# Two of four weight-quarter sums of a seven-product matrix block are made by accumulating DMAs, and modulation rows get four slots instead of two

## The reference, cut to what matters

```
def swiglu_2(h, w_gu, w_down):
    gu = h @ w_gu
    g, u = jnp.split(gu, 2, axis=-1)
    return (jax.nn.silu(g) * u) @ w_down

for l in range(DEPTH_2):
    mod = (c_act @ w_mod[l] + b_mod[l]).reshape(c.shape[0], N_MOD, D_MODEL)
    h = modulate(x, g_norm[l, 0], mod[:, 0], mod[:, 1])
    x = x + 0.5 * mod[:, 2][:, None, :] * swiglu_2(h, w_ffn1_gu[l], w_ffn1_down[l])
    ...                                   # the mixer
    x = x + 0.5 * mod[:, 8][:, None, :] * swiglu_2(h, w_ffn2_gu[l], w_ffn2_down[l])
```

## Time and profile before

| | |
|---|---|
| time, median of 3 runs (range) | 3084.52 us (3080.36 to 3085.5) |
| profiled execution's own time / its span | 3084.16 us / 3082.3 us |
| TensorE busy, share of span | 2865.6 us, 93% |
| VectorE busy | 2375.7 us, 77% |
| ScalarE busy | 1440.6 us, 47% |
| GpSimd busy | 344.7 us, 11% |
| mean granted TensorE clock | 0.978 |
| up halves, first product copied to first down matmul | 211.0, 209.0, 207.6, 209.1 us |
| down halves, first to last down matmul | 149.3, 143.6, 143.0, 120.8 us |

### The profile page before, as it was taken

The page is one execution under the profiler, slowest core; times in us unless marked ns, Lnnn a source line. Parts: engine busy times, 40 slices in busy tenths (PEclk is TensorE's granted clock), DMA queues, the critical chain, the costliest instruction groups (busy, mean ns, idle before and its releaser), DMA issues. The chain is left out here.

```text
span 3082.3 us, 46400 instructions
## 1 busy us (share of the span) xinstructions
PE 2865.6 (93%) x16536; PEld 2396.9 (78%) x16536; DVE 2375.7 (77%) x2913; ACT 1440.6 (47%) x1741; POOL 344.7 (11%) x393
## 2 busy tenths in 40 slices
PE   8999888999999999999989999998999989999998
PEld 4876557777777778897767799876998767789986
DVE  7757758999999978887758688877888666588843
ACT  4125437888888845442146433314333125454421
POOL 0100013333333310101100000010000100000000
PEclk9989999999999999999999999999999999999999
DMA  8552247999999992225631222374223752122221
GB/s 319 169 188 96 90 165 282 368 361 375 373 359 360 368 355 83 95 92 177 235 126 58 80 96 95 117 251 152 94 95 107 252 189 75 63 96 95 94 97 68
DMA packets 115857, 555.68 MB, mean 180 GB/s; under 512 B 20656, under 2 KB 22192, under 8 KB 73776
## 3 DMA queue, kind: packets, MB, share of 16 engines
q1 hardware_dynamic: 89264, 491.43, 43.5%
q0 software_dynamic: 26496, 62.96, 5.7%
HBM read 549.10 MB, written 37.75 MB: 190 GB/s over the span
## 5 line engine op out<-in xcount | busy, mean ns | idle before, releaser
L178 DVE TENSOR_TENSOR stream_low<-stream_raw,stream_high 128x2048 fp32r<-128x2048 f32 x156 | 357.4, 2291 | 254.1 <-ACT stream_high L173 156.0
L173 ACT ACTIVATE stream_high<-stream_raw 128x2048 fp32r<-128x2048 f32 x75 | 143.4, 1913 | 452.7 <-DMA stream_raw<-in_ffn_dn 264.2
L727 ACT ACTIVATE stream_high<-stream_raw 128x2048 fp32r<-128x2048 f32 x76 | 145.5, 1914 | 372.2 <-DVE stream_raw L847 372.2
L473 PE MATMUL ffn_ps_psum<-ffn_t_high,stream_high 128*128 128x256 f32 x912 | 266.8, 293 | 54.6 <-ACT area_f L710 54.6
L473 PE MATMUL ffn_ps_psum<-ffn_pure_high,stream_high 128*128 128x512 f32 x704 | 285.4, 405 | 23.9 <-DVE ffn_pure_low L892 21.5
L317 DVE TENSOR_TENSOR expert_low<-expert_raw,expert_high 128x2048 fp32r<-128x2048 f32 x128 | 292.9, 2289 | 6.3 <-ACT expert_high L313 3.2
L474 PE MATMUL ffn_ps_psum<-ffn_pure_low,stream_high 128*128 128x512 f32 x704 | 278.5, 396 | 0.0
L475 PE MATMUL ffn_ps_psum<-ffn_pure_high,stream_low 128*128 128x512 f32 x704 | 278.1, 395 | 0.0
L475 PE MATMUL ffn_ps_psum<-ffn_t_high,stream_low 128*128 128x256 f32 x912 | 260.9, 286 | 0.0
L474 PE MATMUL ffn_ps_psum<-ffn_t_low,stream_high 128*128 128x256 f32 x912 | 260.8, 286 | 0.0
L313 ACT ACTIVATE expert_high<-expert_raw 128x2048 fp32r<-128x2048 f32 x128 | 244.6, 1912 | 20.4 <-PE experts_g_psum L475 20.4
(11 more groups left out here) (540 smaller groups left out, 7633.8 us busy)
## 6 DMA issues: line engine op xcount, KB each, us to landing
expert_raw<-in_exp_gu SPq DMA_DIRECT2D x128, 1024.0 KB, 9.1
stream_raw<-in_ffn_gu SPq DMA_DIRECT2D x88, 1024.0 KB, 4.8
expert_raw<-in_exp_dn SPq DMA_DIRECT2D x64, 1024.0 KB, 10.7
con<-in_w_mod SPq DMA_DIRECT2D x120, 512.0 KB, 4.3
stream_raw<-in_ffn_dn SPq DMA_DIRECT2D x44, 1024.0 KB, 6.5
mix_mod_rows<-in_w_ada POOLq DMA_DIRECT2D x32, 512.0 KB, 4.4
stream_raw<-in_w_in SPq DMA_DIRECT2D x16, 1024.0 KB, 6.0
pieces_raw<-in_w_in SPq DMA_DIRECT2D x11, 1024.0 KB, 6.3
```

What stands on the lines that cost most here:

```text
L173: self.nc.scalar.activation(self.high[:, q], self.raw[:, q], ACT.Copy).then_inc(self.high_done, 1)
L178: self.nc.vector.tensor_tensor(self.low[:, q], self.raw[:, q], self.high[:, q].bitcast(F32), ALU.subtract)\
L473: mm(out, w[0], x[0], start=start, stop=False)
L727: a(w.high[:, w.slot(s)], w.raw[:, w.slot(s)], ACT.Copy).then_inc(w.high_done, 1)
```

## The change

It has two parts, both in `gated_layer`.

First, the sums. The signs of the scheme are turned (the up columns count as negated), so that all four weight sums are additions: a21+a11, a21+a22, a11+(a21+a22), a12+(that). The first two now come from DMAs. SP loads quarter a21 twice into a new pair buffer `pair_raw` (two slots of 2×512 columns in the corner of `con` where the modulation rows lay), and loads only the other three quarters into `stream_raw`. When the pair has landed, GpSimd issues a DMA that reads a11 and a22 from HBM and adds them into the pair in place. VectorE makes the two remaining sums. The high and low splits of the sums are cut in two halves of 1024 columns: the pair's, and that of the two sums made by VectorE. The reversed sign is taken back by multiplications with −1 in instructions that are there anyway, and by −0.5 for 0.5.

Second, the modulation rows have four slots in the place of `t_high` (T, the sums of activations), which is free in the down half. The order of SP's queue there becomes: a piece, a piece, rows 4 to 7, rows 0 to 3 of the next round.

The diff, cut to its core; in this order SP's loads, SP's down half, ScalarE's split of the sums, GpSimd's adding DMA, VectorE's sums and VectorE's order in `body`:

```diff
                     def up(r, s):
-                        w.load(sp, 2 * r + s, s, w_gu[bass.ds(2 * r + s, 1)].rearrange("a p k n -> (a p) (k n)"))
+                        n, src = 2 * r + s, piece(r, s)
+                        sp.wait_ge(w.low_done, n + (w.base - 1))
+                        sp.dma_start(pair_raw[:, s], src[:, 3 * S:4 * S].unsqueeze(1).broadcast_to([P, 2, S])).then_inc(pair_loaded[s], 16)
+                        sp.dma_start(w.raw[:, w.slot(s), 0:3 * S], src[:, 0:3 * S]).then_inc(w.loaded[w.slot(s)], 16)
...
                         def round_(g):
                             down(g + 1, 0)
-                            mod.load(sp, g, (2, 3, 4, 5))
                             down(g + 1, 1)
-                            mod.load(sp, g, (6, 7))
-                            mod.load(sp, g + 1, (0, 1))
-                        mod.load(sp, 0, (0, 1))
+                            mod.load(sp, g, (4, 5, 6, 7))
+                            mod.load(sp, g + 1, (0, 1, 2, 3))
+                        mod.load(sp, 0, (0, 1, 2, 3))
...
                     def split_sums(r, s):
                         n = 2 * r + s
-                        act.wait_ge(sums_made, 4 * number(n) + 4)
+                        act.wait_ge(pair_summed[s], count(r, s))
                         act.wait_ge(w.used, n + (w.base - 1))
-                        a(w.high[:, w.slot(s)], w.raw[:, w.slot(s)], ACT.Copy).then_inc(w.high_done, 1)
+                        a(w.high[:, w.slot(s), 2 * S:4 * S], pair_raw[:, s].rearrange("p a n -> p (a n)"), ACT.Copy).then_inc(pair_high, 1)
+                        act.wait_ge(sums_made, 2 * number(n) + 2)
+                        a(w.high[:, w.slot(s), 0:2 * S], w.raw[:, w.slot(s), 0:2 * S], ACT.Copy).then_inc(w.high_done, 1)
...
+                    def add_second(r, s):
+                        pool.wait_ge(pair_loaded[s], count(r, s))
+                        nc.gpsimd.dma_start(pair_raw[:, s], w_gu[bass.ds(2 * r + s, 1)].rearrange("a p k (q n) -> (a p) (k q n)", q=2)
+                                            .rearrange("p (b c n) -> p b c n", b=2, c=2)[:, :, 0], accum_op=ALU.add).then_inc(pair_summed[s], 16)
...
                     def make_sums(r, s):
-                        for i, (out, x, y, op) in enumerate(((a22, a21, a22, ALU.add), (a21, a11, a21, ALU.subtract),
-                                                             (a11, a22, a11, ALU.subtract), (a12, a12, a11, ALU.subtract))):
-                            if i:
-                                dve.wait_ge(sums_made, 4 * m + i)
-                            v.tensor_tensor(out, x, y, op).then_inc(sums_made, 1)
+                        dve.wait_ge(pair_summed[s], count(r, s))
+                        dve.wait_ge(pure_low, m + 1)
+                        v.tensor_tensor(a11, a11, pair_raw[:, s, 1], ALU.add).then_inc(sums_made, 1)
+                        dve.wait_ge(sums_made, 2 * m + 1)
+                        v.tensor_tensor(a12, a12, a11, ALU.add).then_inc(sums_made, 1)
...
                         make_sums(*behind)
+                        split_pair(*behind)
                         first_rows(r, s)
-                        w.split_low(dve, *behind)
+                        split_sums(*behind)
                         middle_rows(r, s)
```

More of the change, by code:

```diff
@@ L506, in gated_layer @@
                 hid[:, bass.ds(n, 1), :].rearrange("p a t -> p (a t)")
+            with nc.sbuf_tensor(self.tag + "mod_rows", [P, 4, D], F32) as mod_rows:
+                pass
             t_high, t_low = self.sb("t_high", [P, KD, S], F32R), self.sb("t_low", [P, KD, S], F32R)
@@ L582, in _ @@
                         down(rounds, 0)
-                        mod.load(sp, rounds - 1, (2, 3, 4, 5, 6, 7))
+                        mod.load(sp, rounds - 1, (4, 5, 6, 7))
                     else:
@@ L639, in seven_products @@
                         product(out(six), sums, 0, t_, tok1, 4).then_inc(products, 1)
-                        product(out(seventh), sums, 3, t_, tok1, 0).then_inc(products, 1)
-                        product(out(five), sums, 2, t_, tok0, 0).then_inc(products, 1)
+                        product(out(seventh), sums, 2, t_, tok1, 0).then_inc(products, 1)
+                        product(out(five), sums, 3, t_, tok0, 0).then_inc(products, 1)
                         product(out(three), sums, 1, h, tok1, 4).then_inc(w.used, 1)
@@ L980, in _ @@
                         down(FT // 4 - 1, 1)
-                    v.tensor_scalar(half[:], gate, 0.5, None, mult).then_inc(half_done, 1)
+                    v.tensor_scalar(half[:], gate, -0.5, None, mult).then_inc(half_done, 1)
                     dve.wait_ge(half_done, 1)
```

56 lines of the change are left out of this document (42 added, 14 removed).

## The result

The changed kernel takes 2959.6 us (median of 4 runs, 2947.2 to 2960.3) against 3085.0 us before (3080.4 to 3085.9): ratio 0.9587, 95% interval 0.956 to 0.9614. In a later set it took 2949.9 us (6 runs, 2943.5 to 2964.0), ratio 0.9573 (0.9547 to 0.96). The forecast was 2943. The profiled execution took 2959.1 us.

What follows compares the result with a forecast made beforehand. VectorE was taken to pace the up halves, and waits beside the modulation rows to lengthen three down halves. 3084.2 − 74 (up) − 67.5 (down) = 2942.7, said as 2943 us; range 2920 to 3012, chance 0.70.

Steps and rivals of the forecast that it cites:

- Up halves, direction and mechanism: Up halves: VectorE sets the pace; with two sums instead of four it has 1.5 us slack and TensorE never stops.
- One sign of the wrong: Up halves: VectorE or ScalarE waiting for DMA at the sums in each tile would point to A or B.
- B: Up halves: the add lands at 11 to 14 us, gaining half (2980 us) or nothing (3017); chance 0.08.
- Up halves, size: Four up halves, each falling to 190.1 us: gains of 76 us, taken as 74 for waits near edges.
- the pair's load: Up halves: issued at 8 us of a tile, the load of the pair lands 4.3 us later.
- The add: Up halves: GpSimd's adding DMA lands after 6 us and costs nothing up to 9.4 us.
- Down halves: Three down halves beside modulation: four slots hide the row loads; 73.5 us lost, 67.5 of it gained.
- The two edges: Start and end of each down half beside modulation: first looped piece and L178, priced at 1 us each.
- A: Up halves: add slow or serialised, pair's arrival sets the pace; slower than before, 3279 us at a 20 us add; chance 0.11.
- the point of 12.1: Up halves: the us per tile above which the kernel becomes slower than before, an add landing after 14.9 us.
- C: Down halves: modulation stays short of data, a piece or row late each round; 2983 us; chance 0.08.
- D: Up halves: another producer takes VectorE's place, so TensorE is not freed; 3017 us; chance 0.03.

Runs made afterwards that it cites:

- no add: Changed kernel without the adding DMA, GpSimd only passing the signal on (output not the reference's): 2940.0 us.
- plain write: Changed kernel with GpSimd's DMA of a11 and a22 writing over the pair instead of adding into it (output not the reference's): 2947.6 us.
- early pair: Changed kernel with the pair's load issued 1.9 us sooner, after VectorE's split of the pair two tiles before: 2947.6 us, again 2939.3.
- add-twice: Changed kernel with the add made twice, the second issued when the first has landed (output not the reference's): 3232.4 us.
- sums alone: Changed kernel with the modulation rows back to two slots and the old order of SP's queue: 3028.8 us.
- loads behind the add: Changed kernel where SP issues a tile's two loads only after GpSimd has issued the add of the tile before: 2958.8 us.
- 768 KB first: Changed kernel with SP's two loads of a tile in the other order, the three quarters before the pair: 2941.5 us.

## Why the prediction was right, point by point

**Up halves, direction and mechanism: right.** VectorE's four sums set the pace, two of them moved out free TensorE, and its floor is 190.1 us a half (no add, plain write, early pair). The order on VectorE and its slack came as laid out. One sign of the wrong was there in part, waits for the DMA at the sums, in 25 of 76 tiles on VectorE and 42 on ScalarE: B in small.

**Up halves, size: 63.3 us instead of 74.** The term that was mis-sized is the pair's load. I took 4.3 us from the modulation rows; it is 7.2 to landing and 8.1 to the add's issue. Of that, 6.5 us are there without any add, with 768 KB at once behind a load written twice, and the rest is the add of the tile before, still under way. The issue took 1.07 us instead of 0.53. The add was forecast at 6 us behind its issue, and takes 5.8 to 6 with the issue in it. The way round a slot is 8.1 + 6.0 + 4.6 (copy of the pair to the slot's next load, as in the add-twice timeline) = 18.7 us of 20.16. That leaves 1.4 us where the forecast saw 3.4. It is enough for the median tile. But in most tiles the next tile's loads are issued 1.1 to 2.8 us behind the add. A pair behind such an add is slow (up to 9.3 us from issue to landing), its own add then slips onto the loads after it and lands after 7 to 12 us. The forecast had no such meeting: it held the add to a deadline and the engines to a sum of bytes, and took each transfer's time as fixed. The loss over the floor of 4 × 190.1 us was 13.0 us in the changed kernel, 11.9 in its repeat, 15.1 with the sums alone and 25.1 with the loads behind the add, spread differently over the halves each time, and it goes with the number of adds that took over 10 us: 7, 6, 8 and 9, against one, none and none in early pair, its repeat and 768 KB first, which lost 3.0, 2.0 and 4.6 us.

**Down halves: right, 71.7 instead of 67.5.** The two edges that I priced at 1 us each cost 0.6 us a half together. In the place of TensorE's wait of 9.26 us for L225 at the end of the second half stands one of 0.37 us:

```profile
2050.58 1.12 PE L225 MATMUL ffn_ps_psum<-area_f,ones 128*128 128x512 f32 x2 [0.37 <-DVE area_f L218]
```

What I read into the earlier trace rows was incomplete. VectorE waited for rows just as long (103 us) where the halves were 20 us longer. The pieces caught behind the rows' waits in SP's queue set the time, and the rows' own wait for DMAs doesn't measure it. It came out right because four slots loosen both. The forecast gave the new order a share; beside four slots it has none.

**Elsewhere: 10 us later, not forecast, and not the change's.** The first up half of the changed kernel starts at 1210.9 us, 6.8 later than before, behind code that the change doesn't touch. TensorE's granted clock from 160 to 240 us, before and after:

```profile
160.00:240.00 80.00, 76.35 (x429) 61.55 (x429) 43.20 (x57) 24.17 (x31) 7.49 (x15) 0.88 0.60 205
```
```profile
160.00:240.00 80.00, 75.63 (x384) 61.61 (x384) 38.81 (x53) 19.63 (x27) 6.86 (x13) 0.79 0.53 182
```

Over the profiled executions of all kernels this start goes with the clock of that stretch. Seven have 0.77 to 0.79 there and start at 1210.5 to 1216.5, seven have 0.86 to 0.96 and start at 1200.8 to 1204.3. The changed kernel itself is in both, at 1210.9 once and 1203.4 the other time. So about 7 of the 17 us between forecast and first median are chance; the repeat's median was 2950. What makes the clock dip in one execution and not in another, no run shows. The other 3 us lie between the halves; in the repeat all else together is 0.3 us shorter than before, so they are not the change's either.

**The rivals.** A and B are the same mechanism at two sizes. At the real sizes it sets in now and then (13 us), and with twice the add it outweighs both gains, at 13.9 us a tile, beyond the point of 12.1 that the forecast gave. The engines' share in the up halves, which the forecast put at 0.5 to 0.7, is 0.71 to 0.75. C doesn't occur with four slots. D is refuted by the 190.1. No DMA of GpSimd's was held up by VectorE. The Trainium skill (SBUF — State Buffer, SBUF: two separate sides) names such a stall for VectorE's 2-port modes and infers none for `tensor_tensor`, so the forecast's pure split was not a case of it. The trace agrees: GpSimd's 76 issues of adds took 1.04 to 1.17 us, and the add of 1879.88 stayed out until 1891.6 though VectorE stood idle for the last 6 us of that.

## What to carry to other kernels

Price a new DMA by the transfers issued beside it and not by the landing of an equal size elsewhere. Then add up the whole way round its buffer against the time that the buffers allow. Where little is left, look at which other transfers its issue may meet, and at which it slows itself. If a queue mixes loads that wait for consumers with loads of the critical stream, the number of slots decides how far the stream is held back; reading how late the stream's own pieces are, and how long the queue stands, says more than the side load's wait. Two loads issued together should be tried in both orders.

## What the runs showed of the hardware that I had not expected

- When an add of GpSimd's lands depends on how far ahead of SP's next pair load it was issued (changed kernel and its repeat, to landing). At 1.06 to 5.5 us ahead, 101 adds landed after 5.6 to 6.2 us, but for two at 6.6 and 6.9; at 0.7 to 0.96 us, eleven after 7.3 to 8.9; at less than 0.5 us ahead or up to 0.25 behind, thirteen after 10.4 to 11.7. So 0.6 us of distance are worth up to 5 us.
- An add under way slows the load behind it. The pair landed after 6.5 us with no add at all, and after 8.5 (median of 28) when issued 2 to 3 us behind one.
- 512 KB and 768 KB, issued 0.6 us apart, landed after 6.5 and 7.8 us in this order without an add and 7.2 and 8.7 with one; 768 KB and 512 KB in the other order, with the add, after 4.9 and 6.3.
- For the same 512 KB, an adding DMA took the DMA engines 3.2 us and a plain one 1.56, and GpSimd 1.08 against 0.71 us to issue.
